# Second mixer of a two-layer decoder step: x's sums and the first weight sums ahead of the past rows' columns in VectorE's queue, and four stage tiles for the mixer's output sums

## The chip, the core and the metric

One core of a Trainium2 chip runs the whole step as one program. The time is that of the device, in microseconds, the median of three runs. The engines named here are TensorE (PE: matmuls; PEld: its weight loads), VectorE (DVE), ScalarE (ACT), GpSimd (POOL) and SyncE (SP); each has its own queue and works through it in order, and they wait for each other by semaphores.

## The reference, cut to what matters

Two layers over 512 prompt rows and 8 x 8 sample rows (576 in all, `T`), width 1024. Layer 0 has a gated mixer with spatial weights, layer 1 a short convolution; each is followed by a mixture of experts and a gated projection. The change lies in layer 1's mixer:

```python
h = x @ w_in                                   # 1024 -> 3 * 1024
gate_b, gate_c, hx = jnp.split(h, 3, axis=-1)
hp = jnp.concatenate([past, gate_c * hx], axis=1)
conv = conv_w[0] * hp[:, 0:s]
for k in range(1, 3):
    conv = conv + conv_w[k] * hp[:, k:k + s]
y = (gate_b * conv) @ w_out
x = layer_norm(ALPHA * x + y)
```

All of it is in float32.

## The kernel before

**Splitting.** A float32 operand is kept as two parts of a matmul type, high and low. ScalarE copies a weight unit of 128 x 2048 from `w_raw` to `w_hi` (`hi`, L1054; in two pieces as `first_hi`, L1096 and L1097; `sum_hi`, L1102), VectorE subtracts to get `w_lo` (`lo`, L1509; `first_lo`, L1577 and L1578), and TensorE multiplies high by high, low by high and high by low (L2287, L2288, L2289).

**Seven products in place of eight.** Much of the mixer is computed on 2 x 2 blocks with seven products for a unit of 256 output columns. For this VectorE forms sums of weight blocks (`sums`, L1583 to L1586, in place in `w_raw`) and sums of blocks of x (`combine_x`, L1557, in place in `xT`, four instructions); ScalarE and VectorE split the latter again (`x_combined_hi`, L1451, and `combined_lo_late`, L1566), and VectorE combines the products (`combined`, L1675).

**Order of the mixer.** The orders are written out by hand for each engine. On TensorE: two tiles of gate C's first 256 columns (over `joined(0)` and `joined(1)`, two banks each), the turns of the past rows (`past_turns`, L2906), `h_tiles(0)` and `h_tiles(1)` for hx (each has two halves m, 48 matmuls each, of 256 and 320 columns), then `late_unit(US)`, `late_unit(US + 1)`, `h_tiles(2)` and so on, with products and h tiles in turn. ScalarE copies the C tiles to `c_gate` (`c_copy`, L1436). `conv_mult(f)` on VectorE forms C times hx for feature tile f in `conv_in` (L2165 to L2167), beside the past rows' columns from `pastT`; `conv_taps(f)` forms the three taps (L2176 to L2182). `h_tiles(jj)`, half m, waits before it writes its banks:

```python
if jj:
    pe.wait_ge(cx_ok, 2 * jj - 1 + m)      # conv_mult of the half that used the banks
else:
    pe.wait_ge(c_ok, m + 1)                # c_copy(m)
```

`sum_hi(d)` waits for the sums of its unit and until TensorE has used the unit four before (`wait_used`). For the first summed unit that one is gate C's first.

**Scaled x.** ScalarE writes ALPHA times x to stages (`x_scaled_late`, L1432), GpSimd stores them to `sum_scratch` (L1034). ScalarE's high parts of x's sums wait for all these stores.

**Output sums.** Over the first four feature tiles of g = gate_b * conv, `sum_tiles_late(0)` forms eight tiles of y in turn in two pairs of banks; ScalarE copies each to a stage tile (`sum_copy_late`, L1475) and GpSimd adds it to `sum_scratch` with an accumulating DMA (L941). Tile mo of TensorE waits for the copy of mo - 2, the copy of mo for the store of mo - 2, as they share one of two stage tiles. Afterwards `late_unit(UB + 2)` and `(UB + 3)` follow, then `out_rows(1)`, which turns the sums back to rows (L2530) and adds the last four feature tiles.

Of the kernel before, what the change touches and what calls it, by code (L numbers as in the profile page):

```python
# [7 lines left out]
KT = D // P  # L8
# [3 lines left out]
HALF = T // 2  # L12
# [5 lines left out]
RB, SB = 8, 8  # L18
# [69 lines left out]
def trunk(nc, x_in, outs):  # L88
# [101 lines left out]
    conv = at("conv", [P, KT, T], f32, S0 + 23200)  # L190
    HP = 2 + TP + RB * (2 + SB)
    cx = at("conv_in", [P, 2, HP], f32, S0 + 9216)
# [9 lines left out]
    pastT = at("pastT", [P, KT, RB * 2], f32, S0 + 8704)  # L202
# [128 lines left out]
    with ctx:  # L331
# [158 lines left out]

        def stage_of(mo, late=False):
            k = 2 * (mo % 2)
            return o_stage[0 if late else mo % 4 // 2][:, k:k + 2, HALF:T]

        def u_block(u, m, h, n=1):
# [25 lines left out]
        def c_entry(jj, j):  # L521
            return U_CH + (0, 3, 5, 8)[jj] + j
# [525 lines left out]
        def _(act):  # L1048
# [50 lines left out]
            def sum_hi(d):  # L1099
                act.wait_ge(sums_ok, unit_at(d) + 1)  # L1100
                wait_used(act, d)
                act.activation(unit_of(whi, d), raw_unit(d), ACT.Copy).then_inc(hi_done, 1)  # L1102
# [99 lines left out]
            for l in range(DEPTH):  # L1202
# [220 lines left out]
                if l == 0:  # L1423
                    for k0, k1 in ((0, 4), (4, 7), (7, KT)):
                        act.wait_ge(pe_ok, KT + k1)
                        x_hi(PA, T, k0, k1)

                    def x_scaled_late(k):
                        act.wait_ge(pe_ok, KT + k + 1)
                        if k >= 4:  # L1430
                            act.wait_ge(acc_st[k % 4], ACC_A + 16)
                        act.activation(xs_stage[k % 4 // 2][:, k % 2, :], xk(xT, k, 0, T), ACT.Copy, scale=ALPHA).then_inc(act_scaled, 1)  # L1432

                    def c_copy(m):
                        act.wait_ge(mt_done, M_CH + m + 1)
                        act.activation(c_sb[:, m, :], joined(m), ACT.Copy).then_inc(c_ok, 1)  # L1436

                    for k in range(4):
                        x_scaled_late(k)
                    first_hi(c_entry(1, 0))  # L1440
                    for k in range(4, KT):
                        x_scaled_late(k)
                    for m in range(2):
                        c_copy(m)
                    sum_hi(c_entry(1, 1))
                    for n in range(4):
                        act.wait_ge(acc_st[n], ACC_X)
                    for n, (kh, h) in enumerate(((0, 0), (0, 1), (1, 1), (1, 0))):
                        act.wait_ge(td_ok, 4 + n + 1)
                        for dst, a, b in td_hi_parts(kh, h):  # L1450
                            ins = act.activation(dst[:, :, :], xcols(xT, HALF * h, HALF * h + HALF, 4 * kh + a, 4 * kh + b), ACT.Copy)  # L1451
                        ins.then_inc(tdh_ok, 1)
                    first_hi(c_entry(2, 0))
                    sum_hi(c_entry(2, 1))
                    first_product(US)
                    hi(h_entry(2))
                    first_product(US + 1)
                    first_hi(c_entry(3, 0))
                    sum_hi(c_entry(3, 1))
                    hi(h_entry(3))  # L1460
                    first_product(US + 2)
                    first_hi(b_entry(0, 0))
                    sum_hi(b_entry(0, 1))
                    first_hi(b_entry(0, 2))

                    def g_hi_late(r, fl):
                        q = ROUND * (AR + r) + fl
                        act.wait_ge(gm_done, q + 1)
                        act.activation(halves(ghi[:, fl, :]), g_pair(fl), ACT.Copy).then_inc(gh_done, 1)

                    def sum_copy_late(r, mo):
                        act.wait_ge(mt_done, M_B + KT * r + mo + 1)
                        if mo >= 2:
                            act.wait_ge(acc_st[(mo - 2) % 4], ACC_X + 16 * ((mo - 2) // 4 + 1))
                        act.activation(stage_of(mo, True), pair(mo % 2), ACT.Copy).then_inc(o_done, 1)  # L1475

                    for r in range(BR):
                        first_product(UB + 2 * r)
                        sum_hi(b_entry(r, 3))
                        if r == 0:  # L1480
                            act.wait_ge(last_t, 1)
                            act.activation(last_o[:, :].rearrange("p (b t) -> p b t", b=2), ps[0:18, 0:2, :], ACT.Copy).then_inc(last_cp, 1)
                        hi(b_entry(r, 4))
                        g_hi_late(r, 0)
                        first_product(UB + 2 * r + 1)
                        g_hi_late(r, 1)
                        hi(b_entry(r, 5))
                        g_hi_late(r, 2)
                        g_hi_late(r, 3)
                        if r < BR - 1:  # L1490
                            first_hi(b_entry(r + 1, 0))
                            for mo in range(KT):
                                sum_copy_late(r, mo)
                                if mo == 3:
                                    sum_hi(b_entry(r + 1, 1))
                                if mo == 5:
                                    first_hi(b_entry(r + 1, 2))
                        else:
                            hi(U_P[1])
                            hi(U_P[1] + 1)  # L1500

        @block.vector
        def _(dve):
            ch = Chain(dve, dch)

            def lo(d, it=0, step=0):

                dve.wait_ge(hi_done, it * step + (d + 1))
                dve.tensor_tensor(unit_of(wlo, d), raw_unit(d), unit_of(whi, d).bitcast(f32), ALU.subtract).then_inc(split_done, 1)  # L1509
# [39 lines left out]
            def combine_x(n, late=0):  # L1549
                def part(k, h):  # L1550
                    return xcols(xT, HALF * h, HALF * h + HALF, 4 * k, 4 * k + 4)

                out, a, b, op = ((part(0, 0), part(0, 0), part(0, 1), ALU.subtract),
                                 (part(0, 1), part(0, 1), part(1, 1), ALU.subtract),
                                 (part(1, 1), part(1, 1), part(0, 0), ALU.add),
                                 (part(1, 0), part(1, 0), part(1, 1), ALU.subtract))[n]
                dve.tensor_tensor(out, a, b, op).then_inc(td_ok, 1)  # L1557
                dve.wait_ge(td_ok, 4 * late + n + 1)
# [193 lines left out]
            for l in range(DEPTH):  # L1752
# [395 lines left out]
                if l == 0:  # L2148
                    for n, (k0, k1) in enumerate(((0, 4), (4, 7), (7, KT))):
                        x_low(NT + n, PA, T, k0, k1)  # L2150
                    dve.wait_ge(ws_t, 2)
                    ch.link(dve.tensor_copy(pastT[:, :, :], ps[:, 6, 0:KT * RB * 2].rearrange("p (k c) -> p k c", k=KT)))
                    for m in range(2):
                        ins = dve.memset(cx[:, m, 0:2], 0.0)
                    ch.link(ins)

                    def conv_mult(f):
                        m, jj = f % 2, f // 2
                        if jj:
                            dve.wait_ge(c_done, CS * (US + jj - 1) + 7 + m)  # L2160
                        else:
                            dve.wait_ge(c_ok, m + 1)
                        dve.wait_ge(mt_done, M_CH + 3 + f)
                        own = cx[:, m, 2 + TP:].rearrange("p (b t) -> p b t", t=2 + SB)
                        dve.tensor_copy(own[:, :, 0:2], pastT[:, f, :].rearrange("p (b w) -> p b w", w=2))  # L2165
                        dve.tensor_tensor(cx[:, m, 2:2 + TP], c_sb[:, m, 0:TP], joined(m, 0, TP), ALU.mult)
                        dve.tensor_tensor(own[:, :, 2:], c_sb[:, m, TP:T].rearrange("p (b t) -> p b t", t=SB),  # L2167
                                          joined(m, TP).rearrange("p (b t) -> p b t", t=SB), ALU.mult).then_inc(cx_ok, 1)
# [15 lines left out]
                    def raw_and_sums(d):  # L2184
                        first_lo(d)
                        sums(d)
# [2 lines left out]
                    dve.wait_ge(act_scaled, 2 * KT)  # L2189
                    for n in range(4):  # L2190
                        combine_x(n, 1)
                    lo(c_entry(1, 1))
                    for n in range(4):
                        combined_lo_late(n)
                    conv_mult(0)
                    conv_taps(0)
                    raw_and_sums(c_entry(2, 0))
                    conv_mult(1)
                    conv_taps(1)
                    lo(c_entry(2, 1))  # L2200
                    for n in range(QS):
                        combined(US, n)
# [785 lines left out]
```

## Time and profile before

| | |
|---|---|
| median of 3 runs | 1241.87 us (1241.79 to 1243.19) |
| the profiled execution | 1240.93 us, span 1238.9 us, mean granted clock 0.996 |
| TensorE matmul / weight load | 1197.4 us (97%) / 1082.2 us (87%) |
| VectorE | 956.1 us (77%) |
| ScalarE | 641.9 us (52%) |
| GpSimd | 221.6 us (18%) |
| HBM | 217 GB/s over the span |

The span runs from the first to the last instruction; the time of an execution is somewhat longer. The ends of matmuls are modelled, and each overlaps the next, so distances between starts are what to read. The granted clock is a share of full speed, 2.4 GHz; 0.50 is 1.2 GHz.

### The profile page before, as it was taken

What the parts mean: (1) busy time and instruction counts of PE and PEld (TensorE: products, weight loads), DVE (VectorE), ACT (ScalarE), POOL (GpSimd) and SP (SyncE); (2) the same over time, 40 slices, a digit from 0 to 9 for tenths busy, and PEclk for the clock granted to TensorE, in tenths of its full rate; (3) what the DMA queues carried; (4) which work ended last, traced back from release to release, by engine and by line L of the source; (5) the groups of instructions that cost most, each with busy time, mean ns of one, the idle gap of its engine ahead of it and who ended that gap; (6) DMA issues with size and microseconds to landing.
All of it is one profiled execution on the core that took longest, in us unless ns stands there. A gap on an engine that the chain in (4) does not pass through costs nothing.

```text
span 1238.9 us, 19267 instructions
## 1 busy us (share of the span) xinstructions
PE 1197.4 (97%) x7479; PEld 1082.2 (87%) x7479; DVE 956.1 (77%) x1330; ACT 641.9 (52%) x781; POOL 221.6 (18%) x263
## 2 busy tenths in 40 slices
PE   7999999999999999999999999899999999999998
PEld 6888889999999998788777799799998888877698
DVE  5554888686776868889888885778848889888793
ACT  5232344444354443488787674321342478888662
POOL 3311002131321321122331001000122022232100
PEclk9999999999999999999999999899999999999999
DMA  9456327594866864589997544123386379999522
GB/s 327 142 181 210 118 85 196 120 224 138 174 169 139 208 180 179 176 339 372 369 379 290 203 154 147 35 69 103 112 163 243 145 265 365 386 393 346 212 52 77
DMA packets 104495, 253.57 MB, mean 205 GB/s; under 512 B 10998, under 2 KB 60286, under 8 KB 92128
## 3 DMA queue, kind: packets, MB, share of 16 engines
q1 hardware_dynamic: 71072, 184.56, 42.1%
q0 software_dynamic: 33344, 67.92, 20.0%
q8 instruction: 54, 0.88, 0.3%
q14 instruction: 25, 0.20, 0.0%
HBM read 214.86 MB, written 54.34 MB: 217 GB/s over the span
## 4 chain that ended last, share of the span: by engine, by line
PE 70%; DMA 12%; DVE 10%; ACT 4%; issue 3%; SPq 0%; DVEq 0%; POOLq 0%; ACTq 0%
PE ps L2287 13%; PE ps L2289 13%; PE ps L2288 13%; DMA w_raw<-in_moe_w_gate_up 8%; PE ps L2338 3%; PE ps L2340 3%; PE ps L2339 3%; DVE w_lo L1509 2%; PE ps L2720 2%; PE ps L2722 2%; PE ps L2721 2%; ACT w_hi L1054 2%; PE ps L2541 1%; PE ps L2539 1%; PE ps L2540 1%
## 5 line engine op out<-in xcount | busy, mean ns | idle before, releaser
L1509 DVE TENSOR_TENSOR w_lo<-w_raw,w_hi 128x2048 fp32r<-128x2048 f32 (+1 forms) x133 | 290.8, 2197 | 52.1 <-ACT w_hi L1054 25.9
L1054 ACT ACTIVATE w_hi<-w_raw 128x2048 fp32r<-128x2048 f32 (+1 forms) x114 | 206.6, 1821 | 35.9 <-PE ps L2289 15.2
L2287 PE MATMUL ps<-x_hi,w_hi 128*128 128x288 f32 (+2 forms) x644 | 193.9, 301 | 7.8 <-DVE conv_in L2167 6.1
L2288 PE MATMUL ps<-x_lo,w_hi 128*128 128x288 f32 (+2 forms) x644 | 191.4, 297 | 0.0
L2289 PE MATMUL ps<-x_hi,w_lo 128*128 128x288 f32 (+2 forms) x644 | 191.3, 297 | 0.0
L2287 PEld LDWEIGHTS ps<-x_hi,w_hi 128*128 128x128 f32 x644 | 123.0, 191 | 9.7 <-issue 8.7
L2288 PEld LDWEIGHTS ps<-x_lo,w_hi 128*128 128x128 f32 x644 | 123.0, 191 | 0.0
L2289 PEld LDWEIGHTS ps<-x_hi,w_lo 128*128 128x128 f32 x644 | 122.9, 191 | 0.0
L2287 PE MATMUL ps<-g_hi,w_hi 128*128 128x288 f32 x384 | 114.8, 299 | 3.3 <-ACT out_stage L1475 2.1
L2289 PE MATMUL ps<-g_hi,w_lo 128*128 128x288 f32 x384 | 113.3, 295 | 0.0
L2288 PE MATMUL ps<-g_lo,w_hi 128*128 128x288 f32 x384 | 113.1, 295 | 0.0
L2720 PE MATMUL ps<-w_hi,xgT_hi 128*128 128x512 f32 x256 | 103.1, 403 | 7.4 <-DVE xgT_lo L1925 6.9
L2722 PE MATMUL ps<-w_hi,xgT_lo 128*128 128x512 f32 x256 | 100.2, 391 | 0.0
L2721 PE MATMUL ps<-w_lo,xgT_hi 128*128 128x512 f32 x256 | 99.7, 389 | 0.0
L2288 PE MATMUL ps<-x_combined_lo,w_hi 128*128 128x288 f32 x304 | 89.6, 295 | 0.0
L2287 PE MATMUL ps<-x_combined_hi,w_hi 128*128 128x288 f32 x297 | 88.2, 297 | 0.7 <-DVE w_lo L1509 0.4
L2289 PE MATMUL ps<-x_combined_hi,w_lo 128*128 128x288 f32 x297 | 87.5, 295 | 0.0
L1509 DVE TENSOR_TENSOR w_lo<-w_raw_more,w_hi 128x2048 fp32r<-128x2048 f32 x30 | 68.1, 2292 | 14.2 <-ACT w_hi L1054 14.1
L2338 PE MATMUL ps<-w_hi,x_hi 128*128 128x512 f32 x192 | 75.8, 395 | 1.4 <-DVE x_lo L1528 1.4
L2287 PEld LDWEIGHTS ps<-g_hi,w_hi 128*128 128x128 f32 x384 | 72.1, 188 | 5.9 <-issue 2.3
L2340 PE MATMUL ps<-w_hi,x_lo 128*128 128x512 f32 x192 | 75.4, 393 | 0.0
L2339 PE MATMUL ps<-w_lo,x_hi 128*128 128x512 f32 x192 | 75.3, 392 | 0.0
(364 smaller groups left out, 2774.4 us busy)
## 6 DMA issues: line engine op xcount, KB each, us to landing
w_raw<-in_moe_w_gate_up SPq DMA_DIRECT2D x34, 1024.0 KB, 11.3
w_raw<-in_moe_w_down SPq DMA_DIRECT2D x32, 1024.0 KB, 13.9
w_raw_more<-in_moe_w_gate_up SPq DMA_DIRECT2D x30, 1024.0 KB, 14.8
w_raw<-in_a_w_in SPq DMA_DIRECT2D x23, 1024.0 KB, 5.7
sum_scratch<-out_stage POOLq DMA_DIRECT2D x48, 288.0 KB, 6.3
w_raw<-in_a_w_out SPq DMA_DIRECT2D x12, 1024.0 KB, 6.5
w_raw<-in_b_w_in SPq DMA_DIRECT2D x12, 1024.0 KB, 5.3
w_raw<-in_ple_w_gate SPq DMA_DIRECT2D x8, 1024.0 KB, 12.0
```

The source lines that it names most:

```text
L1054: act.activation(unit_of(whi, d), raw_unit(d), ACT.Copy).then_inc(hi_done, 1)
L1509: dve.tensor_tensor(unit_of(wlo, d), raw_unit(d), unit_of(whi, d).bitcast(f32), ALU.subtract).then_inc(split_done, 1)
L2287: pe.matmul(out, sh, mh, start=first, stop=False)
L2288: pe.matmul(out, sh, ml, start=False, stop=False)
L2289: ins = pe.matmul(out, sl, mh, start=False, stop=final)
L2338: pe.matmul(v_bank(i), xh_, wh, start=first, stop=False)
L2339: pe.matmul(v_bank(i), xh_, wl, start=False, stop=False)
L2340: ins = pe.matmul(v_bank(i), xl_, wh, start=False, stop=final)
L2539: pe.matmul(out, th, wh, start=False, stop=False)
L2720: pe.matmul(ps[:, 0, :], xs[0], ws[0], start=(a == 0 and k == 0), stop=False)
L2721: pe.matmul(ps[:, 0, :], xs[0], ws[1], start=False, stop=False)
L2722: ins = pe.matmul(ps[:, 0, :], xs[1], ws[0], start=False, stop=(a == 1 and k == 3))
```

## The change

On VectorE, what is now `past_columns()` (the copy of the past rows' columns to `pastT` and two small memsets) goes behind the first weight sums and x's sums; `conv_mult(0)` goes ahead of the low parts of x's sums, `conv_mult(1)` ahead of the taps of tile 0, and the taps of tile 1 ahead of the second weight sums. On ScalarE, `sum_hi` of the first summed unit goes ahead of the two `c_copy`. For the output sums of the second mixer, tiles 2, 3, 6 and 7 use rows 0 and 1 of `conv` as a stage, beside the two tiles of `out_stage0` for the others, so a copy waits for the store of four before.

```diff
         def stage_of(mo, late=False):
             k = 2 * (mo % 2)
+            if late and mo % 4 >= 2:
+                return conv[:, mo % 2, :].rearrange("p (h t) -> p h t", t=HALF)
             return o_stage[0 if late else mo % 4 // 2][:, k:k + 2, HALF:T]
...
                     for k in range(4, KT):
                         x_scaled_late(k)
+                    sum_hi(c_entry(1, 1))
                     for m in range(2):
                         c_copy(m)
-                    sum_hi(c_entry(1, 1))
...
                         act.wait_ge(mt_done, M_B + KT * r + mo + 1)
-                        if mo >= 2:
-                            act.wait_ge(acc_st[(mo - 2) % 4], ACC_X + 16 * ((mo - 2) // 4 + 1))
+                        if mo >= 4:
+                            act.wait_ge(acc_st[mo % 4], ACC_X + 16)
...
-                    dve.wait_ge(ws_t, 2)
-                    ch.link(dve.tensor_copy(pastT[:, :, :], ps[:, 6, 0:KT * RB * 2].rearrange("p (k c) -> p k c", k=KT)))
-                    for m in range(2):
-                        ins = dve.memset(cx[:, m, 0:2], 0.0)
-                    ch.link(ins)
+
+                    def past_columns():
+                        dve.wait_ge(ws_t, 2)
+                        ch.link(dve.tensor_copy(pastT[:, :, :], ps[:, 6, 0:KT * RB * 2].rearrange("p (k c) -> p k c", k=KT)))
+                        for m in range(2):
+                            ins = dve.memset(cx[:, m, 0:2], 0.0)
+                        ch.link(ins)
...
                     for n in range(4):
                         combine_x(n, 1)
+                    past_columns()
                     lo(c_entry(1, 1))
+                    conv_mult(0)
                     for n in range(4):
                         combined_lo_late(n)
-                    conv_mult(0)
+                    conv_mult(1)
                     conv_taps(0)
+                    conv_taps(1)
                     raw_and_sums(c_entry(2, 0))
-                    conv_mult(1)
-                    conv_taps(1)
                     lo(c_entry(2, 1))
```

## Rows read from the trace of the kernel before

**Rows 1.** The page, part 1: busy time, share of the span, instructions.
```profile
PE 1197.4 (97%) x7479; PEld 1082.2 (87%) x7479; DVE 956.1 (77%) x1330; ACT 641.9 (52%) x781; POOL 221.6 (18%) x263
```
**Rows 2.** Waits of TensorE, whole span: waiter, releaser, us in total, times, longest.
```profile
PE ps L2287 <- DVE conv_in L2167: 6.1, 1, 6.1
...
PE ps L2287 <- ACT out_stage L1475: 2.1, 1, 2.1
```
**Rows 3.** Timeline of TensorE around the first wait: start, duration, instruction, idle before.
```profile
774.83 0.28 PE L2287 MATMUL ps<-x_hi,w_hi 128*128 128x256 f32 x1
...
781.08 0.31 PE L2289 MATMUL ps<-x_hi,w_lo 128*128 128x320 f32 x1
787.50 0.55 PE L2287 MATMUL ps<-x_hi,w_hi 128*128 128x256 f32 x1 [6.11 <-DVE conv_in L2167]
...
803.03 0.29 PE L2287 MATMUL ps<-x_hi,w_hi 128*128 128x288 f32 x1
```
**Rows 4.** Windows: us, busy PE, PEld, DVE, ACT, POOL; granted clock, DMA, GB/s.
```profile
775.00:781.30 6.30, 6.30 (x48) 6.12 (x47) 6.20 (x4) 5.12 (x6) 0.00 (x0) 1.00 0.01 1
781.30:787.50 6.20, 0.09 (x1) 0.03 (x1) 6.17 (x10) 1.58 (x2) 0.00 (x0) 0.66 0.52 169
787.50:789.50 2.00, 2.00 (x9) 2.00 (x10) 1.93 (x5) 0.00 (x0) 0.00 (x0) 0.50 0.00 0
...
803.10:870.00 66.90, 66.90 (x506) 66.90 (x505) 53.97 (x107) 17.20 (x16) 0.00 (x0) 1.00 0.24 79
...
898.00:900.40 2.40, 0.30 (x3) 0.16 (x2) 0.00 (x0) 0.65 (x1) 0.00 (x0) 1.00 0.98 158
```
**Rows 5.** Timeline of VectorE from its idle time to the second weight unit.
```profile
768.43 0.29 DVE L2152 COPY pastT<-ps 128x128 f32<-128x128 f32 x1 [8.71 <-PE ps L2906]
...
768.90 0.69 DVE L1577 TENSOR_TENSOR w_lo<-w_raw,w_hi 128x512 fp32r<-128x512 f32 x1
...
773.55 5.53 DVE L1557 TENSOR_TENSOR xT<-xT 128x1152 f32<-128x1152 f32 x4
779.11 2.29 DVE L1509 TENSOR_TENSOR w_lo<-w_raw,w_hi 128x2048 fp32r<-128x2048 f32 x1
781.32 4.86 DVE L1566 TENSOR_TENSOR x_combined_lo<-xT,x_combined_hi 128x1152 fp32r<-128x1152 f32 x4
...
786.47 0.17 DVE L2165 COPY conv_in<-pastT 128x16 f32<-128x16 f32 x1
...
805.24 2.29 DVE L1509 TENSOR_TENSOR w_lo<-w_raw,w_hi 128x2048 fp32r<-128x2048 f32 x1 [6.58 <-ACT w_hi L1102]
```
**Rows 6.** Timeline of ScalarE in the same stretch.
```profile
760.70 1.05 ACT L1097 ACTIVATE w_hi<-w_raw 128x1024 fp32r<-128x1024 f32 x1
...
764.05 0.69 ACT L1432 ACTIVATE x_scaled_odd<-xT 128x576 f32<-128x576 f32 x1 [0.23 <-DMA sum_scratch<-x_scaled_odd]
767.40 1.19 ACT L1436 ACTIVATE c_gate<-ps 128x576 f32<-128x576 f32 x2 [2.67 <-PE ps L2289]
773.66 1.92 ACT L1102 ACTIVATE w_hi<-w_raw 128x2048 fp32r<-128x2048 f32 x1 [5.07 <-DVE w_raw L1586]
775.48 3.41 ACT L1451 ACTIVATE x_combined_hi<-xT 128x1152 fp32r<-128x1152 f32 x3
```
**Rows 7.** Timeline of TensorE from the C tiles' last matmul to `h_tiles(0)`.
```profile
767.49 0.31 PE L2289 MATMUL ps<-x_hi,w_lo 128*128 128x320 f32 x1
...
768.33 0.38 PE L2287 MATMUL ps<-x_hi,w_hi 128*128 128x256 f32 x1
```
**Rows 8.** Timeline of TensorE around the second wait, in `sum_tiles_late(0)`.
```profile
897.89 0.29 PE L2289 MATMUL ps<-g_hi,w_lo 128*128 128x288 f32 x1
900.27 0.37 PE L2287 MATMUL ps<-g_hi,w_hi 128*128 128x288 f32 x1 [2.10 <-ACT out_stage L1475]
```
**Rows 9.** Timeline of ScalarE, the third copy; then the eight stores' landing, from `out_stage`'s view.
```profile
899.48 0.65 ACT L1475 ACTIVATE out_stage<-ps 128x576 f32<-128x576 f32 x1 [7.17 <-DMA sum_scratch<-out_stage]
...
DMA to landing us min/median/max: 4.7/6.5/8.3
```

## Prediction

> **What bounds the kernel now.** First the page: TensorE is busy for 1197.4 of 1238.9 us [rows 1], so only what shortens TensorE's own time or fills its gaps can count; the reader is to look at its idle time alone. The waits of TensorE give that by releaser [rows 2]. Two of them lie in the code that the diff touches: 6.1 us, once, for the product `conv_in`, and 2.1 us, once, for a copy into `out_stage`. Then TensorE in order of time around the first of them [rows 3]: the last matmul of `h_tiles(0)` starts at 781.08, the next would follow 0.15 later, at 781.23, and `h_tiles(1)` starts at 787.50. Its 96 matmuls end with the first one of the next unit at 803.03, so they took 15.53 us. The half of `h_tiles(0)` that begins at 774.83 took 6.40 us to 781.23, so the same work at full speed takes 12.80 us. The windows say why [rows 4]: the granted clock is 1.00 up to 781.3, 0.66 on average over the gap and 0.50 (1.2 GHz) in the first 2 us after it. The gap cost 6.27 us in itself, and 15.53 - 12.80 = 2.73 us more in the clock.
>
> Why is `conv_in` late? VectorE in order of time [rows 5] idles 8.71 us, from 759.72 to 768.43, for TensorE's turns of the past rows, and then works without a break through the first weight sums, x's sums (the four `xT` rows), one `w_lo` and `x_combined_lo` before it comes to the product at 786.47. Its input from TensorE was there since about 775. So VectorE's queue sets this gap, and 8.71 us of it was spent waiting at a place where other work was ready.
>
> **Part 1, the past rows' columns behind the sums.** `first_lo` of the first weight sums needs ScalarE's w_hi (L1097), whose instruction starts at 760.70 and takes 1.05, so it ends at 761.75 [rows 6]. From 768.90 to 773.55, `first_lo` and the sums took 4.65 [rows 5]; started at 761.8 they end at 766.5. x's sums wait for ScalarE's last scaled part, 764.05 + 0.69 = 764.74, which is past. They take 773.55 to 779.11, 5.56: they end at 772.0. `past_columns` takes 768.43 to 768.90, 0.47, to 772.5; its wait has been over since 768.4. `lo` of the summed weights takes 779.11 to 781.32, 2.21, to 774.7.
>
> **Part 2, `sum_hi` ahead of the two `c_copy`.** This one costs. `sum_hi` waits for the sums (766.5) and for the unit four before it, which is the one that the first two C tiles read: the last matmul of these starts at 767.49 and lasts 0.31, so 767.8 [rows 7]. In the trace the first copy starts at 767.40 and the pair takes 1.19 [rows 6]. Now `sum_hi` starts at 767.85 and takes 1.92 (L1102), of which 0.1 overlaps the next instruction; the first copy, 0.65 long, runs from 769.65 to 770.3. `h_tiles(0)` waits for that copy: with 0.15 from the copy's end to the first matmul (at the other wait it is 899.48 + 0.65 = 900.13 to 900.27 [rows 8, 9]) it starts at 770.45 instead of 768.33 [rows 7]. New wait: 2.12 us. Queued behind the copy on TensorE is everything. Bounds: 0 if something else held that start anyway (nothing in rows 7 shows it), and 2.12 plus a clock loss like the one seen, 2.73, if the clock falls here too.
>
> **Part 3, `conv_mult(0)` before x's low parts, `conv_mult(1)` before the taps.** `h_tiles(0)` now runs 770.45 to 783.35 (6.50 for the first half, 768.33 to 774.83, and 6.40). `conv_mult(0)` waits for the first half: 776.95 and some 0.15. It takes 0.9 (from 786.47 to 0.15 before TensorE's start at 787.50), so it ends at 778.0 and VectorE stood 2.3 us idle ahead of it, which nothing feels. The low parts (781.32 to 786.47, 5.15) need ScalarE's high parts, of which the first three took 3.41 in all [rows 6]; the four now start at 770.9, right behind the copies, and end by 775.6; so the low parts end at 783.2. `conv_mult(1)` waits for the second half, 783.5, and ends at 784.4. TensorE needs `conv_mult(0)` at 783.35 (5.3 us to spare) and `conv_mult(1)` in the middle of `h_tiles(1)`, at 789.75 (5.3 us too). The gap of 6.27 is gone, and with it the clock's 2.73, and the next unit starts at 783.35 + 12.80 = 796.15 instead of 803.03. That is 6.88 us.
>
> Behind it nothing new is late. The taps and the second sums are the same instructions; VectorE had finished them at 798.66 and then idled 6.58 us [rows 5]. From 781.32 to 798.66 it worked 17.34 without a break; less the low parts (5.15) and two products (0.9 each) that leaves 10.4 for taps and sums. Run from 784.4 they end at 794.8, still 1.4 before ScalarE can take the sums (TensorE's `h_tiles(1)` ends at 796.15). In the next 67 us TensorE has no gap and VectorE is busy 53.97 [rows 4]; all three engines enter this stretch in the same relation as before, 6.88 us earlier, and the weight loads wait for VectorE's splits, so they move along.
>
> **Part 4, four stage tiles.** The stage of output sums 2 and 3 moves to the first two rows of `conv`, whose values are used up by then. In the trace the third copy waits 7.17 us until the first store has landed, starting at 899.48 [rows 9], and TensorE stands from 897.89 + 0.13 = 898.02 to 900.27, and its first matmul back lasts 0.37 where those before took 0.29, so 0.1 more [rows 8]: 2.35 us. With four tiles the third copy waits for its own tile only, near 895, and the fourth follows near 898.2. The fifth needs the first store, landed at 899.4 by the same row, when its own tile is ready near 901.3; the seventh and eighth have their stores, issued near 895.8 and 899.2 and landing 4.7 to 8.3 us later [rows 9], by 904.1 and 907.5, and need them at 907.8 and 911. Bounds: 0 if the stores, now closer together, land over 4 us later; 2.35 otherwise. I take 2.35, since only the first two stores run beside a weight load. The granted clock was 1.00 in this gap [rows 4], so no clock term.
>
> **Sum:** 6.88 + 2.35 = 9.23 us. The profiled execution took 1240.93 us; 1240.93 - 9.2 = 1231.7. The median of the three runs is 0.94 above the profiled one, so the same difference gives 1241.87 - 9.23 = 1232.6.
>
> **Rivals.**
> *The clock falls in the new wait.* Before 770.45 TensorE has 2.1 us idle and, just ahead, only the small transposes of the past rows. For it: the 0.66 over the gap from 781.3 puts the fall only some 2 us into it (a share s at full speed with s + 0.5(1 - s) = 0.66 is s = 0.32, of 6.2 us 2.0). Against: in the 2.3 us gap at 898 it stayed at 1.00 [rows 4]. It would cost up to 2.73 us more: 1235.3. The Trainium skill (TensorE: Matmul & The Clock Gate, Part 1) says that the monitor behind the gate isn't tied to the kernel's start, so that one and the same gap may cost the clock in one execution and not in the next; the two gaps of this trace, of like length up to the fall, agree, and it is why this rival isn't smaller.
> *The stage wait stays.* The stores become the bound: only 6.88, 1235.0.
> *The sums come late and hold the copies.* This ends on the other side. ScalarE's queue now puts VectorE's sums ahead of TensorE's release, so each us by which they end after 767.8 is a us of TensorE. Should VectorE not be able to start before 768.9, where it started before, the sums end at 773.6: the new wait is 2.12 + 5.8 = 7.9, the clock falls as before, and of 11.35 (6.27 + 2.73 + 2.35) only 0.7 is left: 1241.2. With the sums after 774.3 it is slower than before; at 777 it would be 1244.6. Against it: L1097's end at 761.75 and an idle VectorE.
> *Given back later.* VectorE, 81% busy in the 67 us behind, or the first rows' reload, takes back part 1; part 4 remains: 1239.5. Against: the 6.58 us of slack in [rows 5].
>
> **Numbers.** A difference under 0.2% (2.5 us) can't be told from none here. Forecast 0.62; clock falls 0.19; stage wait stays 0.07; given back 0.05; sums late 0.05, of which 0.02 within 0.2% and 0.03 slower; 0.02 for better than forecast. Range: from the new wait costing nothing, 1232.6 - 2.1 = 1230.5, to both small rivals partly at once, 1235.3 + some 1.7 = 1237.0. Faster by over 0.2% are the forecast, the clock, the stage wait, what is better, and half of what is given back: 0.92. Within: 0.05. Slower: 0.03.
>
> **What would show it.** In the profile after: VectorE's first sums from 761.8, ahead of `pastT`; a wait of TensorE for `c_gate` (L1436) near 2.1 us before 770.5; no wait for `conv_in`; granted clock 1.00 through 781 to 796; no wait for `out_stage` (L1475); and `h_tiles(1)` back to 12.8 us. A clock of 0.50 behind 770 would show the first rival, a wait for `c_gate` of over 3 us the third. A start of the sums later than 763 would make the prediction wrong, and so would a wait of TensorE that isn't in the trace now, between 796 and 927.

## The result and the profile after

The changed kernel takes 1233.43 us (median of 4 runs, 1232.95 to 1234.75) against 1242.53 us for the kernel before beside it (4 runs): ratio 0.9929, 95% interval 0.9916 to 0.9941, so 8.8 us less (7.3 to 10.4). Forecast was 1232.6, 9.2 us less.

The two profiled executions are only 6.0 us apart (spans 1238.9 and 1232.9), so the first task is to see what belongs to the change. The waits of TensorE between 745 and 945 us in the profile after are these two:

```profile
PE ps L2292 <- ACT c_gate L1438: 2.1, 1, 2.1
PE ps L2564 <- DVE x_tok L1777: 0.7, 1, 0.7
```

Both waits of [rows 2] are gone; the second row here was there before (0.8 us, just behind this stretch), the first is new. (Lines behind the edit are a few numbers higher: L2292 is L2287 of before, L1438 is L1436.)

VectorE in order of time, in the stretch of [rows 5]:

```profile
762.64 0.69 DVE L1579 TENSOR_TENSOR w_lo<-w_raw,w_hi 128x512 fp32r<-128x512 f32 x1 [2.06 <-ACT w_hi L1099]
...
767.29 5.53 DVE L1559 TENSOR_TENSOR xT<-xT 128x1152 f32<-128x1152 f32 x4
772.85 0.29 DVE L2156 COPY pastT<-ps 128x128 f32<-128x128 f32 x1
...
773.32 2.29 DVE L1511 TENSOR_TENSOR w_lo<-w_raw,w_hi 128x2048 fp32r<-128x2048 f32 x1
779.54 0.17 DVE L2169 COPY conv_in<-pastT 128x16 f32<-128x16 f32 x1 [3.93 <-PE ps L2294]
...
780.70 4.86 DVE L1568 TENSOR_TENSOR x_combined_lo<-xT,x_combined_hi 128x1152 fp32r<-128x1152 f32 x4
...
785.94 0.18 DVE L2169 COPY conv_in<-pastT 128x16 f32<-128x16 f32 x1
...
800.68 2.29 DVE L1511 TENSOR_TENSOR w_lo<-w_raw,w_hi 128x2048 fp32r<-128x2048 f32 x1 [3.60 <-ACT w_hi L1104]
```

This execution is 0.85 us late already ahead of the change (VectorE's split of x starts at 757.62 instead of 756.77). With that taken off, the sums start at 761.8 and end at 766.4, and the columns are copied at 772.0, as the prediction has them. What was an idle 8.71 us is 2.06 us, waiting for ScalarE's w_hi.

ScalarE, in the stretch of [rows 6], has the high part of the summed unit first and the copies behind it:

```profile
768.75 1.91 ACT L1104 ACTIVATE w_hi<-w_raw 128x2048 fp32r<-128x2048 f32 x1 [3.18 <-PE ps L2294]
770.57 1.18 ACT L1438 ACTIVATE c_gate<-ps 128x576 f32<-128x576 f32 x2
771.63 4.08 ACT L1453 ACTIVATE x_combined_hi<-xT 128x1152 fp32r<-128x1152 f32 x4
```

TensorE waits for the first copy. Its timeline, for comparison with [rows 3] and [rows 7], and the windows around it (columns as in [rows 4]):

```profile
768.59 0.66 PE L2911 MATMUL ps<-ident,past_src 16*128 16x16 f32 x8
771.35 0.55 PE L2292 MATMUL ps<-x_hi,w_hi 128*128 128x256 f32 x1 [2.10 <-ACT c_gate L1438]
771.70 0.41 PE L2293 MATMUL ps<-x_lo,w_hi 128*128 128x256 f32 x1
...
774.67 0.28 PE L2292 MATMUL ps<-x_hi,w_hi 128*128 128x256 f32 x1
```

```profile
771.50:774.70 3.20, 3.20 (x16) 3.20 (x17) 3.06 (x5) 3.20 (x4) 0.00 (x0) 0.51 0.00 0
774.70:796.20 21.50, 21.50 (x163) 21.50 (x163) 17.00 (x33) 2.93 (x5) 0.00 (x0) 1.00 0.16 51
```

A matmul of 256 columns lasts 0.41 us at first and 0.28 from 774.67 on. In windows of 0.1 us the granted clock is 1.00 up to 771.2, 0.64 in the next and 0.50 from 771.3 on, so it fell at the very end of the new wait, 0.1 us ahead of the first matmul, and was at 1.2 GHz for some 3.4 us. The forecast had it stay. From 774.7 it is 1.00, through the place where `conv_in` had held TensorE.

The stage tiles do what was read from them. The copies, against [rows 9]:

```profile
886.29 1.45 ACT L1477 ACTIVATE out_stage<-ps 128x576 f32<-128x576 f32 x2 [0.51 <-PE ps L2294]
890.48 0.65 ACT L1477 ACTIVATE conv<-ps 128x576 f32<-128x576 f32 x1 [2.74 <-PE ps L2294]
893.66 0.65 ACT L1477 ACTIVATE conv<-ps 128x576 f32<-128x576 f32 x1 [2.53 <-PE ps L2294]
894.21 1.91 ACT L1104 ACTIVATE w_hi<-w_raw 128x2048 fp32r<-128x2048 f32 x1
896.84 0.66 ACT L1477 ACTIVATE out_stage<-ps 128x576 f32<-128x576 f32 x1 [0.72 <-PE ps L2294]
...
903.20 0.65 ACT L1477 ACTIVATE conv<-ps 128x576 f32<-128x576 f32 x1 [1.06 <-PE ps L2294]
906.38 0.65 ACT L1477 ACTIVATE conv<-ps 128x576 f32<-128x576 f32 x1 [2.53 <-PE ps L2294]
```

Each copy waits for TensorE's tile, none for a store.

**A measure without the drift.** An execution's span moves by a microsecond or more for reasons outside this mixer. So the stretch is measured within each profile, from the start of VectorE's x_lo (756.77 before) to ScalarE's second summed unit (`[rows 5]` names its waiter; 803.29 before), called A, and from there to its high part of `b_entry(1, 4)` (924.58 before), called B. A holds the gap at `conv_in`, B the one at `out_stage`. Before: A 46.52, B 121.29. After: A 798.73 - 757.62 = 41.11, B 917.55 - 798.73 = 118.82. The change took 5.41 + 2.47 = 7.88 us out of these two. The profiled pair shows only 6.0, as this execution of the changed kernel lost 0.85 ahead of A and 1.03 behind B, where nothing was edited (0.85 + 1.03 + 6.0 = 7.88).

### The profile page after: what moved, and what is told of

It reads as the page before. It is cut to its first block, busy times and chain, and to the rows that moved or that the text cites. A ratio compares the mean times of both kernels' runs of the same rounds, so it can differ in the third digit from the quotient of the medians.

```text
span 1232.9 us, 19265 instructions
## 1 busy us (share of the span) xinstructions
PE 1196.5 (97%) x7479; PEld 1081.3 (88%) x7479; DVE 956.3 (78%) x1330; ACT 641.5 (52%) x781; POOL 219.6 (18%) x263
## 4 chain that ended last, share of the span: by engine, by line
PE 72%; DMA 12%; DVE 9%; ACT 4%; issue 3%; SPq 0%; DVEq 0%; POOLq 0%; ACTq 0%
PE ps L2292 14%; PE ps L2294 13%; PE ps L2293 13%; DMA w_raw<-in_moe_w_gate_up 9%; PE ps L2343 3%; PE ps L2344 3%; PE ps L2345 3%; PE ps L2725 2%; DVE w_lo L1511 2%; PE ps L2727 2%; PE ps L2726 2%; ACT w_hi L1056 2%; DMA x_gathered<-y_scratch 1%; PE ps L2546 1%; PE ps L2545 1%
## 5 line engine op out<-in xcount | busy, mean ns | idle before, releaser
L2292 PE MATMUL ps<-x_hi,w_hi 128*128 128x288 f32 (+2 forms) x644 | 193.3, 300 | 3.9 <-ACT c_gate L1438 2.1
L2292 PEld LDWEIGHTS ps<-x_hi,w_hi 128*128 128x128 f32 x644 | 122.4, 190 | 5.7 <-issue 4.5
L2292 PE MATMUL ps<-g_hi,w_hi 128*128 128x288 f32 x384 | 114.6, 298 | 1.2 <-DVE g_lo L1663 1.0
L2292 PE MATMUL ps<-x_combined_hi,w_hi 128*128 128x288 f32 x297 | 88.3, 297 | 0.7 <-DVE w_lo L1511 0.4
L2292 PEld LDWEIGHTS ps<-g_hi,w_hi 128*128 128x128 f32 x384 | 72.1, 188 | 3.5 <-DVE g_lo L1663 2.0
```

The lines of the kernel that those rows point to most:

```text
L2292: pe.matmul(out, sh, mh, start=first, stop=False)
```

## The experiments

All in one table first; "turns to h" is the time from the start of the past rows' turns to the first matmul of `h_tiles(0)`. "Less than before" is from the ratio with its 95% interval, times 1241.3 us. The kernel before ran beside each group of experiments (1241.2 to 1241.4) and beside the changed kernel's first runs (1242.53).

| kernel | A | B | A + B against before | turns to h | median us | less than before, us |
|---|---|---|---|---|---|---|
| before | 46.52 | 121.29 | | 0.60 | 1241.2 to 1241.4 | |
| changed (three profiles) | 41.11, 41.13, 41.15 | 118.82 to 118.84 | -7.88 | 2.76 | 1233.43, 1233.53, 1233.19 | 8.8, 8.3, 8.1 |
| stage_only | 45.88 | 118.81 | -3.12 | 0.59 | 1238.60 | 2.9 (1.7 to 4.0) |
| queues_only | 39.64 | 121.07 | -7.10 | 2.76 | 1235.51 | 5.1 (3.5 to 6.8) |
| cols_early | 46.71 | 118.84 | -2.26 | 8.52 | 1239.83 | 1.9 (0.7 to 3.0) |
| cols_late_only | 39.12 | 118.82 | -9.87 | 0.59 | 1232.59 | 9.7 (8.1 to 11.4) |
| products_only | 41.67 | 115.95 | -10.19 | 0.60 | 1231.53 | 10.7 (8.9 to 12.3) |
| filler (two profiles) | 39.66, 39.66 | 118.82 | -9.33 | 2.77, 2.76 | 1232.43, 1233.36 | 9.2, 8.7 |
| copy_first (two profiles) | 37.52, 37.52 | 118.83, 118.82 | -11.46 | 0.60, 0.59 | 1230.32, 1230.24 | 11.7, 11.2 |

**The copies first.** The changed kernel with one move undone:

```diff
+for m in range(2):
+    c_copy(m)
 sum_hi(c_entry(1, 1))
-for m in range(2):
-    c_copy(m)
```

> The changed kernel with ScalarE's two gate C copies back ahead of the summed unit's high part; all else as changed. Theory A (the parts add as read from the rows): TensorE's 2.1 us wait for c_gate goes, and with it the fall of the clock that the changed kernel's profile shows there (3.4 us at 1.2 GHz, about 1.5 us lost). No wait takes its place, since the next thing that TensorE needs of this stretch, the first product, has some 5 us to spare. So 11.35 us less than before, about 1231.2, and 2.1 to 3.6 us less than the changed kernel. Rival B (the summed unit's high part must be early, or the low part of it holds VectorE and the first product): a wait for conv_in of 1 to 2 us appears and the time stays within 1 us of the changed kernel's 1233.4.

Measured: 1230.32 us, 11.7 us less than before (9.8 to 13.5). It was run once more beside the changed kernel on one chip:

> The kernel with the gate C copies first, once more, on one chip with the two below. Theory A: 2.1 us of wait and the clock's share less than the changed kernel: 2.1 us where the clock stayed, 3.6 where it fell, so 2.1 to 3.6 us apart by the medians. Rival B (the difference of 3.1 us between the medians seen so far was the chips'): under 1.5 us apart.

> The changed kernel, on one chip with its two neighbours. Theory A: 8 to 9.5 us less than before, and in its profile the wait for c_gate of 2.1 us, with or without 3.4 us at 1.2 GHz behind it.

Measured there: 1230.24 us against 1233.19, 2.95 us apart. ScalarE in its second profile:

```profile
767.60 1.19 ACT L1438 ACTIVATE c_gate<-ps 128x576 f32<-128x576 f32 x2 [2.66 <-PE ps L2294]
768.68 1.92 ACT L1104 ACTIVATE w_hi<-w_raw 128x2048 fp32r<-128x2048 f32 x1
770.49 4.08 ACT L1453 ACTIVATE x_combined_hi<-xT 128x1152 fp32r<-128x1152 f32 x4
```

and VectorE, which now needs that high part:

```profile
772.66 2.29 DVE L1511 TENSOR_TENSOR w_lo<-w_raw,w_hi 128x2048 fp32r<-128x2048 f32 x1
775.30 0.17 DVE L2169 COPY conv_in<-pastT 128x16 f32<-128x16 f32 x1 [0.35 <-PE ps L2294]
```

The high part is ready at 770.6 and its low part starts at 772.66, without a wait: `sum_hi` ahead of the copies buys nothing, and it cost TensorE 2.16 us (2.76 - 0.60) and the clock. Between 745 and 800 TensorE waits for nobody in this kernel. It beats both kernels and is the best version found.

**The stage tiles alone.** The kernel before with the two edits to `stage_of` and `sum_copy_late`.

> The kernel before with the four stage tiles alone. Theory A: the 2.35 us at TensorE's wait for out_stage, and nothing else, about 1240.2. Rival B (accumulating stores bound this stretch anyway, or the first rows' reload behind it does): under 1 us less than before.

Measured: B falls by 2.48. A falls by 0.64 too, with the same wait of 6.1 us for `conv_in`, as the clock came back sooner in this execution: matmuls of 256 columns last 0.41 us from 788.71 to 792.55, and 0.28 from 792.96 on. TensorE worked some 4.5 us at 1.2 GHz behind the wait, where it was 6.0 in the kernel before (787.50 to 793.5). So one and the same gap cost 2.73 us in the clock in one execution and 2.73 - 0.64 = 2.09 in the other. The median is 2.9 us less, its interval holds 2.35.

**The queues alone.** The changed kernel with two stage tiles.

> The changed kernel with the two stage tiles of before. Theory A: 6.9 us less than before without a fall of the clock in the new wait and 5.4 with one, so 1235.6 to 1237.1; the 2.1 us wait for out_stage is back. Rival B (part of what the queues give is taken back behind them, and the stage tiles gave more than their own wait): less than 4.5 us.

Measured: 1235.51. Its profile has the same wait for `c_gate`, and yet the clock stayed. TensorE and the windows:

```profile
769.09 0.66 PE L2909 MATMUL ps<-ident,past_src 16*128 16x16 f32 x8
771.85 0.36 PE L2290 MATMUL ps<-x_hi,w_hi 128*128 128x256 f32 x1 [2.10 <-ACT c_gate L1436]
```

```profile
768.00:771.80 3.80, 1.75 (x16) 1.46 (x15) 3.73 (x3) 2.55 (x3) 0.00 (x0) 1.00 0.17 64
771.80:775.20 3.40, 3.35 (x27) 3.39 (x28) 3.23 (x6) 3.40 (x4) 0.00 (x0) 1.00 0.00 0
```

So A is 39.64, which is 46.52 - 6.88: to the hundredth the sum of parts 1 to 3 for a clock that stays. The last digits are luck, since they hold against the very execution that the 2.73 us were read from; against stage_only's A the difference is 6.24. Against the changed kernel's 41.13 it prices the fall: 1.49 us.

**Work in the wait.** The changed kernel with eight matmuls over ones into an unused bank:

```diff
 past_turns()
+for _ in range(8):
+    pe.matmul(ps[:, 5, :].rearrange("p (a t) -> p a t", t=P), ones_r[:, :],
+              ones_r[:, :].unsqueeze(1).to_broadcast([P, 4, P]), start=True, stop=True)
 h_tiles(0)
```

> The changed kernel with eight matmuls of 512 columns over a tile of ones into an unused bank, between the past rows' turns and the first h tile, so within TensorE's 2.1 us wait for c_gate (8 x 0.22 = 1.8 us); their result is used by nothing. Theory A (the fall of the clock in that wait is a cost of its own, in most executions): the wait shrinks to some 0.4 us, the first h tile starts no earlier, the clock stays at 1.00, and the time is up to 1.5 us less than the changed kernel's. Rival B (the clock falls there only in the odd execution, such as the profiled one): the median is that of the changed kernel within 0.5 us.

> The changed kernel with the eight idle matmuls in the wait, on one chip with it. Theory A: the clock stays at 1.00 in its profile, and it lies between the changed kernel and the one with the copies first: 2.1 us above the latter, 0.5 to 1.5 us below the former. Rival B (the clock falls too seldom to show): within 0.5 us of the changed kernel.

Measured, in the first profile:

```profile
769.83 2.09 PE L2952 MATMUL ps<-ones_r 128*128 128x512 f32 x8
772.00 0.35 PE L2292 MATMUL ps<-x_hi,w_hi 128*128 128x256 f32 x1
```

```profile
772.00:775.40 3.40, 3.40 (x28) 3.40 (x29) 3.23 (x6) 3.40 (x4) 0.00 (x0) 1.00 0.02 5
```

The h tile starts no earlier (2.77 and 2.76 after the turns), the clock stays at 1.00, and A is 39.66 in both profiles, some 1.5 less than in the three of the changed kernel. In the medians this doesn't show clearly: about 1 us less than the changed kernel's on other chips, and 0.2 more than it on the same chip. The second profile lost 2.4 us more than the first behind B, with a wait of 2.7 us for gathered rows in the experts' part, where the first had 1.0, and a granted clock of 0.86 and 0.80 in the 10 us around and behind it (985 to 995); other runs may have had the like.

How often the fall is paid can be bounded from the mean granted clock, which is on record for every execution, profiled or not. One fall of 3.4 us takes 1.7 of 1232 us, so the mean reads 0.999 at most; and of the 13 profiled executions the five that read 1.000 have no fall ahead of the last 20 us, and the eight that read less have one. A reading below 1.000 doesn't say where the clock fell. Of the changed kernel's 14 executions four read 1.000: the clock did not fall there. So the fall is paid in at least 3 and at most 10 of 14. In the three kernels with the copies first 14 of 19 read 1.000, in the filler kernel 8 of 10, in queues_only 2 of 5. This is what one expects if the wait makes the fall likely and the filler prevents it. In the changed kernel's two later groups the six executions below 1.000 took 1234.1 us on average and the four at 1.000 took 1232.7, though falls elsewhere have a part in that.

**The rival with late sums.** The changed kernel with `past_columns()` ahead of `raw_and_sums(c_entry(1, 0))`.

> The changed kernel with the past rows' columns back ahead of the first weight sums, where VectorE waits for TensorE's turns; ScalarE's summed unit stays ahead of the gate C copies. This is the state of the rival in which the sums come late. Theory A: the sums end near 773.6, the copies follow ScalarE's 1.9 us, TensorE waits 7.9 us for c_gate, the clock falls as before: about 1 us less than before, 1241 to 1242. Rival B (the order of the columns hardly matters, the products' places do): the time stays within 2 us of the changed kernel's 1233.4.

Measured, in TensorE's waits and on ScalarE:

```profile
PE ps L2292 <- ACT c_gate L1438: 7.9, 1, 7.9
```

```profile
773.67 1.91 ACT L1104 ACTIVATE w_hi<-w_raw 128x2048 fp32r<-128x2048 f32 x1 [8.91 <-DVE w_raw L1588]
775.49 1.17 ACT L1438 ACTIVATE c_gate<-ps 128x576 f32<-128x576 f32 x2
```

ScalarE stands 8.91 us for the sums, and TensorE the predicted 7.9 behind it. Nearly all of the change's gain is gone by one place in one queue: 1.9 us less than before, where I had expected about 1. A is 0.19 longer than before, and what is left is the stage tiles' 2.45 in B. The clock fell here too and cost 1.27 us (46.71 - 46.52 + 9.00 for the old gap and its clock - 7.92 for the new wait), not the 2.73 of before.

**One move at a time, copies first.** The kernel with the copies first, once with the columns early again, once with the products and taps back in their places:

```diff
 # products_only
+past_columns()
 raw_and_sums(c_entry(1, 0))
...
-past_columns()
 lo(c_entry(1, 1))
```

```diff
 # cols_late_only
 lo(c_entry(1, 1))
-conv_mult(0)
 for n in range(4):
     combined_lo_late(n)
-conv_mult(1)
+conv_mult(0)
 conv_taps(0)
-conv_taps(1)
 raw_and_sums(c_entry(2, 0))
+conv_mult(1)
+conv_taps(1)
```

> The columns back ahead of the first weight sums and the copies back ahead of the summed unit's high part, so of the queue changes only the places of the first two products and the taps are kept; with the four stage tiles. Theory A: the first product follows the low part of the summed weights, at 781.3, and TensorE waits some 1.1 us for it in place of 6.1; the clock need not fall. 11.35 - 1.1 = 10.3 us less than before, about 1232.2, so less than the changed kernel although two of its moves are undone. Rival B (the idle 8.7 us of VectorE is what counts): the gap stays near 5 us and the time is over 1237.

> The columns behind x's sums, the copies ahead of the summed unit's high part, and the products and taps in their places of before; with the four stage tiles. Theory A: the low parts of x's sums end at 779.9, the first product at 780.8, just in time for the second h tile; the second product ends at 789.2 behind the second weight sums, and TensorE waits 1.6 us for it in the middle of that tile. 11.35 - 1.6 = 9.7 us less than before, about 1232.8. Rival B (one place alone gives back little): over 1236.

> The changed kernel once more, beside the three above on one chip. Theory A: 9.2 us less than before; its profile shows whether the clock falls in the wait for c_gate again. If the fall comes in one execution and not in another, the clock is 1.00 through this wait here or the stretch at 1.2 GHz has another length than 3.4 us; if it is tied to the wait, it falls at the same place.

Measured, TensorE's rows with a wait, of the first and of the second:

```profile
783.45 0.36 PE L2292 MATMUL ps<-x_hi,w_hi 128*128 128x256 f32 x1 [0.96 <-DVE conv_in L2171]
```

```profile
789.80 0.38 PE L2292 MATMUL ps<-x_hi,w_hi 128*128 128x256 f32 x1 [1.33 <-DVE conv_in L2171]
```

Expected were 1.1 and 1.6, and 10.3 and 9.7 us less than before; A + B gives 10.19 and 9.87, the medians 10.7 and 9.7. (In products_only ScalarE's second summed unit, where A ends, waits for VectorE's sums and not for TensorE, so A is longer and B shorter by the same amount, and only their sum is to be read.) The columns' place and the products' place are two cures for one gap: each alone, with the copies first and the four stage tiles, gives more than the changed kernel, which pays for `sum_hi`, and together they add 1.3 to 1.6 us to one of them (11.46 in all). The changed kernel, run again beside them, took 1233.53, and the clock fell again (A 41.13), but at another place than in the first profile:

```profile
771.21 0.36 PE L2292 MATMUL ps<-x_hi,w_hi 128*128 128x256 f32 x1 [2.10 <-ACT c_gate L1438]
771.40 0.28 PE L2293 MATMUL ps<-x_lo,w_hi 128*128 128x256 f32 x1
...
772.11 0.32 PE L2293 MATMUL ps<-x_lo,w_hi 128*128 128x256 f32 x1
772.23 0.41 PE L2294 MATMUL ps<-x_hi,w_lo 128*128 128x256 f32 x1
```

The clock was 1.00 through the whole wait and for 1.0 us of matmuls behind it, and fell only at 772.2, again for 3.4 us. By what I had written down, 1.00 through the wait would speak against a tie to it; I hadn't thought of a fall right behind it. In the third profile it fell 0.1 us behind the wait's end. So in three profiles the wait is followed by a fall of the same length and price, though not at the same moment.

## Why the prediction was right, and where it was not

- **The gap at `conv_in` (parts 1 and 3, 6.27 + 2.73):** right. The wait is gone and, but for the new wait at `c_gate`, nothing in A or B took its place. The 2.73 for the clock is one execution's number; in stage_only the same gap cost 2.09.
- **The new wait (part 2, 2.12 us):** right in place and size, 2.16. That the sums are done when ScalarE wants them (766.5 against 767.85) held; the rival that they aren't was built and gave the 7.9 us it was priced at; of the gain it left 2.3 us in A + B and not 0.7, as the clock cost 1.27 us there and not 2.73.
- **6.88 us for parts 1 to 3 with a clock that stays:** 6.88 in queues_only, 6.86 in the filler's two profiles, each against the profile that the prediction was read from.
- **The clock in the new wait:** this is the step that failed. I took 1.00, with a chance of 0.19 for a fall. It fell in all three profiles of the changed kernel, at the wait's end or up to 1.0 us behind it, and stayed in that of queues_only, whose wait is the same; by the mean clocks it stayed in four other executions of the changed kernel. The fall costs 1.47 to 1.49 us, not the 2.73 taken as its upper bound, since TensorE worked at 1.2 GHz for at most 3.4 us and not for 6.0. 9.23 - 1.47 = 7.76 against 7.88 in A + B. So what the three profiles show is the first rival, at about half the price that I gave it, and 0.19 was too low for it. Whether this is why the median, 1233.43, lies 0.8 us above the forecast isn't shown: the measured 8.8 us less has an interval of 7.3 to 10.4, which holds 9.23 as well as 7.76. The sentence drawn from the Trainium skill (TensorE: Matmul & The Clock Gate, Part 1), that one and the same gap may or may not cost the clock, agrees with these four profiles and with the mean clocks; the weight that I drew from it was too small.
- **The stage tiles (2.35 us):** 2.47 (B), and 2.48 alone. The 0.1 more is a second small pause, before the seventh tile, which I had left out.
- **Nothing given back later:** right. B is 118.8 in every kernel with four tiles in which the queues enter it alike, and VectorE's sums are done at 797.08 (800.68 less the 3.60 of idle time), 1.65 us before ScalarE takes them at 798.73, where 1.4 had been worked out.

What the prediction didn't ask is whether `sum_hi` had to move at all. Its own numbers had the answer: the low part of that unit runs at 772.5, ScalarE could have the high part ready by 770.5 behind the copies (767.40 + 1.19 + 1.92), and the 2.12 us stood in the sum as a cost without a return.

## What to carry to other kernels

A wait in a queue is worth what stands ready behind it: move the waiting instruction behind ready work, and the instruction that TensorE waits for ahead of work that nobody is late for. Ask the second question for every moved instruction, and of each engine's queue: who needs it first, and who is now behind it? Of two cures for one gap the second adds little, so price each alone with the other in place. And compare stretches between two fixed instructions within each profile; here they repeat to 0.04 us where the clock does the same, while the medians of one kernel were up to 0.9 us apart (filler) and could not show 1.5.

## What the runs showed of the hardware

A wait of TensorE of 2.1 us, with eight small transposes (0.66 us) just ahead of it, was followed by a fall of the clock to 1.2 GHz in three profiles and not in a fourth with the same wait. The fall came 0.1 us ahead of the wait's end in one of the three, and 0.1 and 1.0 us behind it in the others, when full-width matmuls were running again. It lasted 3.4 us and cost 1.5 us each time. The waits of 2.1 and 2.0 us for `out_stage`, with full-width matmuls right up to them, left the clock at 1.00 in both profiles that have one (the kernel before and queues_only). Whether the transposes make the difference was not tested.

In the wait of 6.1 us for `conv_in`, which the kernel before and stage_only share, the clock fell 2.1 us into it in one execution and 4.0 in the other, and cost 2.73 and 2.09 us behind it (A 46.52 and 45.88). With the wait of 7.9 us in cols_early it cost 1.27: the longer wait did not cost more in the clock.

Full-width matmuls whose result nobody reads, set into the 2.1 us, went with a clock of 2.4 GHz in both profiles and a mean of 1.000 in 8 of 10 executions, against 4 of 14 without them, and delayed the work behind by nothing (2.77 and 2.76 us against 2.76).
